# Hybrid DeltaNet and differential attention step: where a map's first transposes stand against the second side product

## The reference, cut to what matters

```python
# DeltaNet, in chunks (the kernel uses chunks of 128 tokens), per head
m   = einsum('ik,jk->ij', k*beta, k) * decay
a   = where(i > j, m, 0) + eye
u,w = triangular_solve(a, [v*beta, k*beta*exp(gcum)])
v_new = u - w @ S
o   = (q*exp(g)) @ S + (q @ k.T * decay) @ v_new
S   = S*exp(g_last) + (k*exp(g_last - g)).T @ v_new
# differential attention, per head and block of 128 queries
A1, A2 = causal softmax maps of the two 64-wide halves
out = (A1 - lam * A2) @ v
```

## Time and profile before

| | |
|---|---|
| median of 3 runs | 1739.94 us (1737.72 to 1742.2) |
| profiled execution | 1741.67 us, span 1740.1 us |
| TensorE matmuls in flight | 1619.8 us (93%) |
| TensorE weight loads | 1539.0 us (88%) |
| VectorE, ScalarE, GpSimd busy | 991.6, 524.9, 312.2 us |
| mean granted TensorE clock | 0.974 |
| merged stage | 425 to 711 us of the span |

### The profile page before, as it was taken

How to read it: one execution, slowest core, us unless ns; L and a number is a source line. 1 busy time by engine, 2 the same in 40 slices (tenths; PEclk the granted TensorE clock), 3 DMA queues, 4 the chain that set the end, 5 groups by cost and what they waited for, 6 DMA issues and landing times.

```text
span 1740.1 us, 27805 instructions
## 1 busy us (share of the span) xinstructions
PE 1619.8 (93%) x10602; PEld 1539.0 (88%) x10602; DVE 991.6 (57%) x1417; ACT 524.9 (30%) x810; POOL 312.2 (18%) x717
## 2 busy tenths in 40 slices
PE   5999999898799999687699999999999999999998
PEld 5899999898588888463599999999999999999997
DVE  4454379786566565346334655565565555655654
ACT  4243332332344343422322322121121221211214
POOL 2200056554432432332000000000000000000000
PEclk9999999999899999889799999999999999999999
DMA  4311111232113211453512121011020210110104
GB/s 144 124 49 48 37 50 41 75 99 81 37 40 86 67 40 24 133 216 104 168 57 61 37 69 53 24 60 57 27 60 12 72 49 24 60 60 24 48 0 110
DMA packets 151572, 114.29 MB, mean 66 GB/s; under 512 B 26027, under 2 KB 139197, under 8 KB 150070
## 3 DMA queue, kind: packets, MB, share of 16 engines
q1 hardware_dynamic: 145842, 101.35, 19.6%
q0 software_dynamic: 2304, 8.39, 1.4%
q10 hardware_dynamic: 3350, 3.53, 0.6%
HBM read 90.59 MB, written 21.74 MB: 65 GB/s over the span
## 4 chain that ended last, share of the span: by engine, by line
PE 49%; DVE 1%; ACT 1%; issue 0%; DMA 0%; SPq 0%; ACTq 0%; DVEq 0%
PE f_up L2958 28%; PE f_down L2965 14%; PE f_up L181 4%; PE f_up L2918 1%; PE f_up L2945 1%; PE f_up L2965 0%; PE f_up L3003 0%; DVE h_rstd L2798 0%; DMA f_rows<-in_ffn_conv_b 0%; DVE o_lo L2778 0%; PE f_up L2992 0%; PE f_down L2908 0%; ACT f_tail_tok L2726 0%; DVE w_lo L2747 0%; DVE dn_lo L2889 0%
## 5 line engine op out<-in xcount | busy, mean ns | idle before, releaser
L2958 PE MATMUL f_up<-h_hi,w_hi 128*128 128x352 f32 x1032 | 335.1, 325 | 1.9 <-DVE w_lo L2747 1.2
L2958 PE MATMUL f_up<-h_hi,w_lo 128*128 128x352 f32 x1032 | 333.4, 323 | 0.0
L2958 PE MATMUL f_up<-h_lo,w_hi 128*128 128x352 f32 x1032 | 333.4, 323 | 0.0
L181 PE MATMUL proj<-x_hi,win_hi 128*128 128x352 f32 x672 | 220.7, 328 | 5.3 <-issue 3.0
L181 PE MATMUL proj<-x_hi,win_lo 128*128 128x352 f32 x672 | 217.9, 324 | 0.0
L181 PE MATMUL proj<-x_lo,win_hi 128*128 128x352 f32 x672 | 217.7, 324 | 0.0
L2958 PEld LDWEIGHTS f_up<-h_hi,w_hi 128*128 128x128 f32 x1032 | 193.8, 188 | 2.5 <-DVE w_lo L2747 1.5
L2958 PEld LDWEIGHTS f_up<-h_hi,w_lo 128*128 128x128 f32 x1032 | 194.1, 188 | 0.0
L2958 PEld LDWEIGHTS f_up<-h_lo,w_hi 128*128 128x128 f32 x1032 | 193.7, 188 | 0.0
L2965 PE MATMUL f_down<-f_g_hi,dn_hi 128*128 128x352 f32 x512 | 165.3, 323 | 0.0
L2965 PE MATMUL f_down<-f_g_hi,dn_lo 128*128 128x352 f32 x512 | 164.7, 322 | 0.0
(11 more groups left out here) (439 smaller groups left out, 2941.0 us busy)
## 6 DMA issues: line engine op xcount, KB each, us to landing
w_raw<-in_w_up SPq DMA_DIRECT2D x44, 512.0 KB, 3.9
win_raw<-in_w_in SPq DMA_DIRECT2D x28, 512.0 KB, 4.0
dn_raw<-in_w_down SPq DMA_DIRECT2D x11, 1024.0 KB, 5.1
p_key<-in_cache_k SPq DMA_DIRECT2D x32, 256.0 KB, 3.8
feat<-in_cache_v POOLq DMA_DIRECT2D x24, 256.0 KB, 5.7
x_scratch<-feat SPq DMA_DIRECT2D x1, 4224.0 KB, 13.4
feat<-x_scratch SPq DMA_DIRECT2D x8, 528.0 KB, 9.0
feat<-in_x_prompt SPq DMA_DIRECT2D x8, 512.0 KB, 8.1
```

Of the source, the lines that this page charges most:

```text
L181: mm = nc.tensor.matmul(out, w[:, k, :], x[:, k, g * TG:(g + 1) * TG], start=(k == 0 and i == 0), stop=(k == KT - 1 and i == 2))
L2958: mm = nc.tensor.matmul(up[u % RING][:, 0:TG], a[s][:, kk, :], b, start=(kk + x == 0), stop=(kk == KT - 1 and x == 2))
```

## The change

In every period `turn_map(last, 0)` is issued behind the second side product and not ahead of it. In the periods before chunk 0 it goes behind `spread_beta`, `keys_queries` and `spread_decay` likewise. The other engines keep their order, and no instruction, wait or transfer is added or taken away.

```diff
@@ tensor engine, in the loop over plan
                         extend(n, p)
                     else:
                         solve_w(n)
-                if last is not None:
-                    turn_map(last, 0)
                 t = chunk_at(n, p, "spread_beta", 3, 2)
                 if t is not None:
                     spread_beta(t)
...
                     spread_decay(t)
                 if n >= 1 and p == 0:
                     state_next(n - 1)
+                if last is not None:
+                    turn_map(last, 0)
                 if last is not None and groups_of(last) == 2:
                     turn_map(last, 1)
                 t = chunk_at(n, p, "turn_values", 3, 1)
```

## The result

| | median of the runs | profiled execution (span) | merged stage | samples | mean clock |
|---|---|---|---|---|---|
| before | 1739.91 us | 1741.67 (1740.1) | 286.8 | 130.0 | 0.974 |
| after | 1772.15 us | 1769.94 (1768.4) | 312.5 | 134.7 | 0.965 |

The changed kernel is slower: the ratio after to before is 1.0172 (95% interval 1.0147 to 1.0198, 4 runs of each), so 30 us; the medians lie 32.2 apart. The forecast was 1760.2 with a range to 1769; the direction is right, the size too small by a third. I compare profiled executions: forecast 1762.0, measured 1769.9.

What follows compares the result with a forecast made beforehand. TensorE, full and in program order, bounds the merged stage. Terms 9.8 + 6.7 + 0.2 + 1.6 + 2.0 = 20.3 us on the profiled 1741.67 gave 1762.0, or 1760.2 for the median; range 1751 to 1769.

Steps and rivals of the forecast that it cites:

- What the product covers: Between first transposes and what awaits their copy, the product's 0.89 us is free: 1.45 us with or without it.
- Plain periods: Eleven periods (seven `keys_queries`, three `state_next`, chunk 4's `spread_decay`): transposes start 0.89 us later each, 9.8 us together.
- Spread_decay with two groups: Five third periods: 1.46 us each in chunks 1, 3, 5, 1.15 each in chunks 0 and 2; 6.7 us together.
- Fourth periods: Six periods where `turn_values` waits for `c_AT`: little time comes back, sum +0.2 us, lowest -2.7.
- Late `c_vn`: `state_next` in first periods waits for delayed `c_vn`: 0.73 us in chunk 1, 0.72 in 3, 0.2 in 2; sum 1.6.
- Before chunk 0: Three periods ahead of chunk 0: late exponentials delay `keys_keys` and maps, `keys_queries` gains 0.6; sum +2.0 us, 0 to +3.
- The clock: Rival: clock falls in the merged stage's new gaps, four stretches of 1.7 us, so 6.8 more, 1767.0 us; chance 0.20.
- The stages before and after it as now: Sign expected in the profile: only the merged stage grows, to some 306 us; its neighbouring stages keep their length.
- faster: Rival: TensorE's waits for `a_e` and `c_AT` (5.8 and 6.9 us) are all covered, giving 1727 us; chance 0.05.
- no change: Rival: the diagonal blocks' round through DRAM and GpSimd to `join` paces the merged stage, giving 1740 us; chance 0.06.
- half of it: Rival: ScalarE and VectorE absorb delays and fourth periods gain, giving 1751.5 us; chance 0.12.

Runs made afterwards that it cites:

- The four parts: Kernel before with only second, only third, only first and fourth, or only the pre-chunk-0 periods changed: ratios 1.0057, 1.0069, 1.0033, 1.0025.
- the same 15.1 us of work: Needless matmuls before the second transposes or map-value product in 17 periods: ratio to before 1.0053 in the kernel before, 1.0126 in the changed kernel.
- the filled kernel: Changed kernel plus 4 needless matmuls (0.89 us) where the product stood, in 17 periods: ratio 1.0126 to the kernel before.
- the delays in the kernel before: Kernel before with 4, 8 or 12 needless matmuls ahead of the merged stage's last `state_w`: sample stage 135.2, 132.9 and 135.4 us.

## Why the prediction was wrong

It gave 20.3 us and 28.3 came in the profile (30 in the runs). By its own steps:

- **What the product covers.** Right. It was the cover of ScalarE's first copy. The four parts, and the same 15.1 us of work at 10.0 us in one order and 0.5 in the other, show it. The Trainium skill, page "Perfetto Trace Analysis", section "Identifying the Most-Contended Engine", would have the load's busy share taken and not the matmul's. It speaks of busy shares; no run here tests that, and that the trace sides with the page, as the prediction has it, goes further than the page. The nearest thing in the runs is the idle columns: the periods grew by 0.93 to 0.95, near the 0.89 of the product and the 0.97 of idle loads, and not by the 0.73 of the matmuls' column.
- **Plain periods**, 0.89 each: seven with `keys_queries` 6.13 us (6.23 forecast), the other four as forecast within 0.1.
- **Spread_decay with two groups.** 1.46 forecast for each of chunks 1, 3, 5; 1.38 and 1.39 with only these periods moved, 1.59 in chunk 1 in the whole change. 1.15 for chunks 0 and 2; 1.21 and 1.20. In chunk 3 of the whole change VectorE's step added 0.9, which the sum did not have.
- **Fourth periods**: +0.2 forecast; -0.1 with only them and the first moved (-0.08 - 0.22 - 0.08 - 0.06 + 0.32). **Late `c_vn`**: 1.68 and 1.69 for the first periods of chunks 1 and 3 where 1.62 and 1.61 were forecast, 0.94 in chunk 2 where the assumed 0.2 did not come. **Before chunk 0**: 2.2, forecast 2.0, but the agreement is luck: some 0.8 of the 2.2 is the clock's, and the moved work cost about 1.4.
- **The clock**, the step that failed. The sum has nothing for it. Against the rival I argued "at 519 us two waits of 0.41 and 0.84 us stand as close, and the clock stayed at 1.00" and gave it 0.20. But the moved transposes were what parted those two waits: with them gone they, and the transposes' time, are one wait, 1.77 us in chunk 1 (526.19), 2.69 and 1.85 in chunks 3 and 5, followed by the new wait for the copy. In chunks 3 and 5 the clock fell, in both profiles of the changed kernel, and in chunk 1 it did not. In the merged stage the clock cost 5.2 us: 3.7 and 2.3 for these two, 0.8 before chunk 0, less the 1.6 of the old stretch that is gone. The rival's price, four stretches at 1.7 us, so 6.8, came near the 6.0 of the two by luck: they were fewer and longer, and it forgot the 1.6.
- **"The stages before and after it as now"** failed as well, for the samples: +4.7 us in the profiles. Neither the sum nor any rival had it. The two only together leave the range: 1760.2 + 5.2 = 1765.4 lies within it, and with 4.7 more it is 1770.1, above 1769. The clock rival's 1767.0 would have become 1771.7, close to the 1772.15 measured.
- The two other rivals, faster and no change, fell; "half of it" too.

Forecast 20.3, its terms -0.7, VectorE's step 0.9, clock in the merged stage 5.2, samples 4.7, first and last stage -2.1: 28.3 us.

Left open: why the clock fell at 597.3 and 665.5 and not after the like waits in chunk 1, nor at 599.6 in the filled kernel; why it fell in chunk 5 in the kernel with only the second periods changed; and what lengthens the sample stage. A later start of it fits the delays in the kernel before and does not fit the filled kernel, so it is not shown.

## What to carry to other kernels

In an engine that is full and works in order, the price of moving a block is found by comparing start to start of its neighbours in periods with it and without it: here 1.45 us both ways, so the block was free, and once it no longer stands in that wait its full 0.89 us comes on top. Ask of every block that is moved out from between two waits whether they become one, and where they do put a price for the lower clock into the sum: here it was 2.3 to 3.7 us in two places of three, though waits in two pieces did not keep the clock up everywhere either. Ask also what the shifted engines will now run beside: 0.9 us came from a VectorE step that had met no long GpSimd step before. And where a later stage with much idle time follows, let the range hold some 5 us for its clock, whatever is changed ahead of it: eighteen profiles gave 129.6 to 135.9 us for one and the same stage.

## What was not expected of the hardware

An untouched stage took 129.6 to 130.0 us in three profiles, with 41.8 to 45.2 us of it at a granted clock of 0.50, and 132.2 to 135.9 us in fifteen profiles of kernels edited elsewhere, with 56.8 to 65.1 us at 0.50. A VectorE step of 0.69 us took 1.58 to 2.30 beside a GpSimd step of 1.26 us and ended 0.49 us after it, four times of four. And 184 more weight loads, with their matmuls, made the eight chunks 5.2 us shorter than the changed kernel without them, since the clock stayed at 1.00. And equal executions of one kernel spread over 12 us (1737.5 to 1749.5), with the mean clock between 0.975 and 0.965.
